# Reordering twelve attention input panels so that four attention pairs run among them, and splitting the first two output panels in halves

## The reference, cut to what matters

```
q, k, v = split(rms_norm(x) @ w_in)     # 16 query heads of 64, 4 key and 4 value heads
for each block b of 128 tokens:          # 4 blocks
    keys of block b and of block b - 1 (block 0 has none before it)
    s = q.k / 8 - slope[head] * distance, outside the band: -inf
    m = max(max(s), sink[head])
    p = exp(s - m);  denom = sum(p) + exp(sink - m)
    o = (p / denom) @ v
x = x + concat(o) @ w_out                # the output projection
x = x + swiglu(rms_norm(x))
```

## Time and profile before

| | us |
|---|---|
| median of three runs | 2536.35 |
| the profiled execution, its own time | 2536.2 |
| its span in the trace | 2534.4 |
| panel 7 to panel 11 | 2012.5 to 2041.2 |
| from panel 11's end to the first output panel | 2041.2 to 2107.3 |
| the eight output panels | 2107.3 to about 2151 |

### The profile page before, as it was taken

How to read it: one execution, slowest core, us unless ns; L and a number is a source line. 1 busy time by engine, 2 the same in 40 slices (tenths; PEclk the granted TensorE clock), 3 DMA queues, 4 the chain that set the end, 5 groups by cost and what they waited for, 6 DMA issues and landing times.

```text
span 2534.4 us, 35089 instructions
## 1 busy us (share of the span) xinstructions
PE 2441.7 (96%) x12016; PEld 2072.3 (82%) x12016; DVE 1682.5 (66%) x3142; ACT 928.1 (37%) x1319; POOL 740.1 (29%) x646
## 2 busy tenths in 40 slices
PE   6999999898999999999999999999999979999998
PEld 4877878686887888888888899999999756788886
DVE  4887769688566667677642478888887685444434
ACT  4223853523233333333333333333333464222222
POOL 0000000000006666676676257777641000000000
PEclk8999999999999999999999999999999999999999
DMA  6222913254234444444456689999997202222321
GB/s 257 100 73 93 350 34 129 95 190 159 100 111 139 139 148 141 150 138 149 139 171 193 206 295 366 365 366 362 360 363 258 76 25 67 91 99 91 100 99 58
DMA packets 177221, 433.59 MB, mean 171 GB/s; under 512 B 32752, under 2 KB 81904, under 8 KB 176752
## 3 DMA queue, kind: packets, MB, share of 16 engines
q1 hardware_dynamic: 123888, 331.61, 37.8%
q0 software_dynamic: 34816, 67.41, 7.7%
q10 hardware_dynamic: 18432, 33.56, 3.6%
HBM read 371.48 MB, written 61.01 MB: 171 GB/s over the span
## 4 chain that ended last, share of the span: by engine, by line
PE 87%; DVE 9%; ACT 2%; issue 1%; DMA 1%; SPq 0%; ACTq 0%; DVEq 0%
PE ps L466 17%; PE ps L467 17%; PE ps L468 17%; PE ps L802 9%; PE ps L803 9%; PE ps L801 9%; PE ps L712 2%; DVE wlo L1398 1%; DVE ar L1451 1%; PE ps L696 1%; PE ps L704 1%; PE ps L781 1%; DVE ar L1513 1%; ACT whi L936 1%; DVE rstd L1412 1%
## 5 line engine op out<-in xcount | busy, mean ns | idle before, releaser
L1398 DVE TENSOR_TENSOR wlo<-raw,whi 128x1024 fp32r<-128x1024 f32 x426 | 521.4, 1224 | 569.7 <-ACT whi L936 568.2
L2239 POOL DMA_INDIRECT w_scratch<-ar x384 | 418.8, 1091 | 953.5 <-DVE wlo L1398 854.3
L936 ACT ACTIVATE whi<-raw 128x1024 fp32r<-128x1024 f32 x424 | 448.9, 1059 | 660.0 <-PE ps L803 403.4
L466 PE MATMUL ps<-b_hi,whi 128*128 128x512 f32 x1328 | 519.6, 391 | 3.2 <-DVE wlo L1398 3.0
L468 PE MATMUL ps<-b_hi,wlo 128*128 128x512 f32 x1328 | 517.6, 390 | 0.0
L467 PE MATMUL ps<-b_lo,whi 128*128 128x512 f32 x1328 | 517.3, 390 | 0.0
L801 PE MATMUL ps<-a_hi,whi 128*128 128x384 f32 x1024 | 342.7, 335 | 0.0
L803 PE MATMUL ps<-a_hi,wlo 128*128 128x384 f32 x1024 | 342.1, 334 | 0.0
L802 PE MATMUL ps<-a_lo,whi 128*128 128x384 f32 x1024 | 342.1, 334 | 0.0
L466 PE MATMUL ps<-a_hi,whi 128*128 128x512 f32 x816 | 326.9, 401 | 8.9 <-DVE wlo L1398 7.2
L467 PE MATMUL ps<-a_lo,whi 128*128 128x512 f32 x816 | 319.6, 392 | 0.0
(11 more groups left out here) (265 smaller groups left out, 2988.7 us busy)
## 6 DMA issues: line engine op xcount, KB each, us to landing
raw<-panels SPq DMA_DIRECT2D x430, 512.0 KB, 3.4
gelu_scratch<-ar ACTq DMA_DIRECT2D x128, 256.0 KB, 2.1
w_scratch<-rstd SPq DMA_DIRECT2D x32, 768.0 KB, 10.9
ar<-w_scratch SPq DMA_DIRECT2D x128, 192.0 KB, 4.7
ar<-gelu_scratch SPq DMA_DIRECT2D x128, 192.0 KB, 5.6
ar<-mod SPq DMA_DIRECT2D x32, 512.0 KB, 5.6
ar<-panels SPq DMA_DIRECT2D x3, 2048.0 KB, 16.0
w_scratch<-ar POOLq DMA_INDIRECT x384
```

Of the source, the lines that this page charges most:

```text
L466: pe.matmul(bank, w_h, hi[:, k, :], start=(k == 0), stop=False)
L936: act.activation(whi[:, u % SPLIT, :], raw[:, u % RAW, :], ACT.Copy).then_inc(hi_ready, 1)
L1398: dve.tensor_tensor(wlo[:, u % SPLIT, :], raw[:, u % RAW, :], f32(whi[:, u % SPLIT, :]), ALU.subtract).then_inc(lo_ready, 1)
L2239: nc.gpsimd.indirect_dma_start(experts, bass.IndirectOffsetOnAxis(offs[:, k:k + 1], 0), vals[:, k:k + 1], None)\
```

## The change

The panels' order becomes key 0, value 0, queries 0 to 3, key 1, value 1, queries 4 to 7. From the seventh on all use bank 3, and each waits until the one before it has been taken out. Groups are ordered by kt outside and b from 3 down to 0 inside, so pairs 0 to 3 need only the first seven panels. Their work is written among panels 7 to 11, on all three engines. The first two output panels are each split into two halves of four tiles; the first halves need only the outputs of kt = 0 and are written among pairs 6 and 7. Output panels use banks 4 to 7. The maximum's three short instructions become two, with `less_sinks` made once. `v2_feat_sb` moves into `nt`.

```diff
-SWB = (0, 2, 3, 1)
+SWB = (0, 2, 3, 1, 0, 2, 3, 3, 3, 3, 3, 3)
+SW_ORDER = (0, 2, 4, 5, 6, 7, 1, 3, 8, 9, 10, 11)
-        v2_feat_sb = area(A_S2, 2, T)
+        v2_feat_sb = nt[:, :, :]
@@ SP
+            for n, w in enumerate(SW_ORDER):
+                sp.wait_ge(lo_ready, SW + n - RAW + 1 - U)
+                sp.dma_start(raw[:, (SW + n) % RAW, :], panels[SW + w]).then_inc(landed[(SW + n) % RAW], 16)
...
+            groups = [(b, kt, half) for kt in range(2) for b in reversed(range(TT)) for half in range(2)]
...
@@ PE
+            swa_panel(6)
+            swa_scores(0)
+            swa_panel(7)
             swa_scores(1)
+            swa_panel(8)
+            swa_turn(0)
+            turn_v(1, 2)
+            swa_scores(2)
+            swa_turn(1)
+            swa_panel(9)
+            swa_values(0)
+            swa_turn(2)
+            swa_scores(3)
+            swa_turn(3)
+            swa_panel(10)
+            swa_turn(4)
+            swa_values(1)
+            swa_turn(5)
+            swa_panel(11)
+            swa_turn(6)
+            pe.wait_ge(bank_free, r_of(SW) + 16)
+            swa_scores(4)
+            swa_values(2)
+            swa_turn(7)
+            swa_scores(5)
+            swa_values(3)
+            swa_turn(8)
+            swa_scores(6)
+            swa_turn(9)
+            swa_scores(7)
+            swa_turn(10)
+            swa_values(4)
+            swa_turn(11)
+            swa_turn(12)
+            swa_values(5)
+            out_half(0, 0)
+            swa_turn(13)
+            swa_turn(14)
+            swa_values(6)
+            out_half(1, 0)
+            swa_turn(15)
+            swa_values(7)
+            out_half(0, 1)
+            out_half(1, 1)
...
@@ ACT
+            for n in range(4):
+                bias_tiles(n)
+                swa_panel_hi(6 + n)
+            bias_tiles(4)
             swa_exp(0)
             swa_exp(1)
+            swa_panel_hi(10)
+            swa_exp(2)
+            swa_exp(3)
+            swa_out(0)
+            swa_panel_hi(11)
+            swa_out(1)
+            swa_exp(4)
+            swa_exp(5)
+            swa_hi(0)
+            swa_out(2)
+            swa_panel_hi(12)
+            swa_out(3)
+            swa_exp(6)
+            swa_exp(7)
+            bias_tiles(5)
+            swa_out(4)
...
+            swa_out(10)
+            swa_exp(12)
+            swa_hi(4)
+            hi_next(0, SO, 0)
...
-                dve.tensor_tensor(tiny[:, o:o + 4], tiny[:, o:o + 4], col("sinks", h, 4), ALU.max).then_inc(mx2, 1)
-                dve.wait_ge(mx2, n + 1)
-                dve.tensor_scalar(tiny[:, o + 4:o + 8], tiny[:, o:o + 4], -1.0, None, ALU.mult).then_inc(nmx2, 1)
-                dve.tensor_tensor(tiny[:, o + 12:o + 16], col("sinks", h, 4), tiny[:, o:o + 4], ALU.subtract).then_inc(nmx2, 1)
+                dve.scalar_tensor_tensor(tiny[:, o + 4:o + 8], tiny[:, o:o + 4], -1.0, less_sinks[:, h:h + 4], ALU.mult, ALU.min).then_inc(nmx2, 1)
+                dve.wait_ge(nmx2, 2 * n + 1)
+                dve.tensor_tensor(tiny[:, o + 12:o + 16], col("sinks", h, 4), tiny[:, o + 4:o + 8], ALU.add).then_inc(nmx2, 1)
...
@@ DVE, after panel 11
+            pair_bias(4)
+            swa_lo(2)
+            pair_bias(5)
+            pair_norm(4)
+            pair_bias(6)
+            swa_lo(3)
+            pair_norm(5)
+            pair_bias(7)
+            lo_next(0, SO, 0)
+            swa_lo(4)
+            pair_norm(6)
+            swa_lo(5)
+            pair_norm(7)
+            swa_lo(6)
+            swa_lo(7)
```

More of the change, by code:

```diff
@@ L175, in build @@
         tiny = sb("tiny", [P, 96])
+        less_sinks = sb("less_sinks", [P, NH2])
         sq = sb("sq", [P, 2, T])
@@ L909, in _, with out_half @@
-            pe.wait_ge(o2, len(groups) // 2 - 1)
-            strips(SO, KT, b_hi, b_lo, each=last_outputs)
+            def out_half(u, half):
+                if half == 0:
+                    pe.wait_ge(lo_ready, SO + u + (1 - U))
+                    pe.wait_ge(bank_free, r_of(SO) + u + 1)
+                    pe.wait_ge(bias2, 4 * len(groups))
+                    pe.wait_ge(o2, TT)
+                else:
+                    pe.wait_ge(o2, 2 * TT)
+                for k in range(4 * half, 4 * half + 4):
+                    last = split3(ps[:, 4 + u, :], u, k, b_hi[:, k, :], b_lo[:, k, :], k == 0, k == KT - 1)
+                if half:
+                    last.then_inc(used, 1)
@@ L912, in last_stat @@
+            out_half(1, 1)
+            for k in range(2, KT):
+                panel(SO + k, k % 4, ps[:, 4 + k % 4, :], b_hi, b_lo, r_of(SO) + k + 1)
             def last_stat(i, u):
@@ new lines, in query2, with residual @@
+            def query2(n, p):
+                dve.wait_ge(used, SW + p + 1)
+                dve.scalar_tensor_tensor(q2[:, n, :], ps[:, SWB[p], :], HD2 ** -0.5, rstd[:, :], ALU.mult, ALU.mult).then_inc(bank_free, 1)
+            def residual(first, count):
+                for n in range(first, first + count):
+                    dve.scalar_tensor_tensor(x[:, n, :], x[:, n, :], col("final1", n), rstd1, ALU.mult, ALU.mult).then_inc(y1_ready, 1)
+            swa_panel_lo(1)
+            norm_rstd(3)
@@ L2058, in _ @@
+            swa_panel_lo(2)
+            key2(0, 0)
+            swa_panel_lo(3)
+            value2(0, 1)
+            swa_panel_lo(4)
             for k in range(1, KT - 1):
                 add_sq(4, k, rstd1)
[L2060 to L2064, removed]
+            query2(0, 2)
@@ L2066, in swa_bias @@
+            value2_out(0, 4)
+            swa_panel_lo(5)
+            query2(1, 3)
+            groups = [(b, kt, half) for kt in range(2) for b in reversed(range(TT)) for half in range(2)]
             def swa_bias(n):
@@ L2118, in _, with pair_bias, pair_norm @@
[L2118 to L2121, removed]
+            def pair_bias(m):
+                swa_bias(2 * m)
+                swa_bias(2 * m + 1)
+            def pair_norm(m):
                 swa_norm(2 * m)
                 swa_norm(2 * m + 1)
[L2124 to L2128, removed]
@@ L2129, in _ @@
-            swa_lo(len(groups) // 2 - 1)
+            query2(2, 4)
+            dve.tensor_scalar(less_sinks[:, :], col("sinks", 0, NH2), -1.0, None, ALU.mult).then_inc(mx2, 1)
+            swa_panel_lo(6)
+            norm_rstd(4, rstd1)
+            query2(3, 5)
+            swa_panel_lo(7)
+            residual(0, 4)
+            key2(1, 6)
+            swa_panel_lo(8)
+            dve.wait_ge(mx2, 1)
+            dve.wait_ge(bias_ready, NH2 // 2)
+            pair_bias(0)
+            value2(1, 7)
```

176 lines of the change are left out of this document (98 added, 78 removed).

## The result

The changed kernel takes 2545.62 us, the median of six runs (2543.74 to 2546.84); before, run beside it, takes 2536.27 (six runs, 2536.1 to 2540.2). The ratio is 1.003, with a 95% interval of 1.0018 to 1.0041: slower by 9.4 us, some 5 to 10. The forecast was 2544.5 in a range of 2538 to 2549. The profiled execution took 2545.18 us, with a span of 2543.4. One of the ten executions of a later experiment, keep_warm, took 4398.79 us at a mean granted clock of 0.705 and stands in no comparison.

What follows compares the result with a forecast made beforehand. Attention was taken as a chain through three engines, none full, held back by ACT's written order. Order 5.6 later plus clock 2.6 gave 8.2 us on the profiled 2536.2, 2544.5 by the median; range 2538 to 2549.

Steps and rivals of the forecast that it cites:

- Before panel 7: Start of the stage: panel 6 ends 1.9 us earlier, as waits for a value panel and a `lo` go.
- Panels 7 to 11: Attention work among these panels: 44.8 us of PE work plus 10.9 of waits with restarts, 55.7 in all.
- turn 3: PE's wait there: exponentials 4 and 5 and the rest take ACT 5.5 us against PE's 4.1, 1.35.
- nearly 7: ACT's idle us before `hi` 11, waiting for panel 9, with a copy and exponentials behind; the same expected at `hi` 12.
- After panel 11: Rest of attention: 25.1 us of work and 18.4 of waits with restarts, 43.5 without output work.
- The clock and the sum: PE's slower clock at 5.5 places, 5.7 us against 3.1 before, adds 2.6; with 5.6 the total is 8.2 slower.
- the order's part: Attention's end, output work left out: 2109.8 against 2104.2 for before by the same reckoning, 5.6 us later.
- The first: Rival: ACT reaches copies 1 and 3 and exponentials during panels 9 and 10; 4.9 us faster, 2531.5; chance 0.11.
- The second rival: Panels around the waits keep PE's clock up: only 2.5 us slower, 2538.9; chance 0.13.
- The third: Rival: every long PE wait drops the clock: 15.3 us slower, 2551.7; chance 0.08.
- The short instruction: One of DVE's three short maximum instructions goes: 0.08 us off each group, bounds 0 to 2.7 over 16 groups.
- The one bank for panels 7 to 11: Claimed to cost nothing: DVE's taking out lies under attention work, showing only as 0.4 us at scores 4.

Runs made afterwards that it cites:

- keep_warm: Changed kernel plus 79 extra matmuls with unread results in eight PE waits of about 2 us or more; stage 197.94 us, ratio to before 1.0023.
- changed_again: The changed kernel run once more, unmodified, on another chip; stage 201.80 us, ratio to before 1.0022.
- act_order: Changed kernel with ACT's whole written order in the attention stage redone, PE and DVE untouched; stage 185.59 us, ratio to before 0.9978.
- the second pair: Both kernels, before and changed, run once more unmodified on another chip; stages 196.88 and 201.80 us.
- outs_first: Changed kernel with ACT's copies of groups 1 and 3 moved ahead of the `hi` of panels 11 and 12; stage 202.85 us, ratio to before 1.0046.
- exps_first: As outs_first, with exponentials 0 also ahead of `hi` 9 and exponentials 4 and 5 ahead of `hi` 11; stage 200.14 us, ratio to before 1.0026.
- all_order: Changed kernel with the written orders of PE, ACT and DVE in the attention stage all renewed; stage 173.13 us, ratio to before 0.9901.
- order_no_halves: As all_order, with the output panels undivided and behind the last pair; stage 175.65 us, ratio to before 0.9915.

## Why the prediction was right

**Before panel 7.** Panel 6 ends 47.7 after the first input panel began, before 49.6: 1.9 earlier, as forecast.

**Panels 7 to 11.** 57.9 against a forecast of 55.7 without the clock. The waits, forecast then measured: turn 0 0.3 and none, turn 1 2.4 and 2.94, values 0 2.25 and 2.12, turn 3 1.35 and none, turn 4 2.25 and 2.21, turn 5 2.0 and 2.03. Turn 3's is missing because values 0 in front of it ran at half speed (3.32 in place of 1.94), which used it up. In changed_again, where values 0 ran at full speed, it is there:

```profile
2097.25 1.94 PE L892 MATMUL ps<-ar 128*64 128x512 f32 x8 [2.12 <-ACT ar L1381]
...
2102.85 1.07 PE L872 MATMUL ps<-sm,ar 128*128 128x128 f32 x8 [1.54 <-ACT ar L1381]
```

ACT stood 6.79 before `hi` 11 and `hi` 12, forecast "nearly 7". That the waits come from ACT's order was argued there and is shown by act_order: the same work in 45.1. The Trainium skill (TensorE: Matmul & The Clock Gate, Architectural detail) has ScalarE strictly first in, first out; the trace agrees with it by those two waits of 6.79, in the last 5.6 of which a ready copy stood behind.

**After panel 11.** 53.0, less 5.4 of output halves, is 47.5, against 43.5 without the clock. Waits, forecast then measured: scores 4 0.4 and 0.35, scores 5 0.9 and 1.03, turn 8 4.3 and 4.32, scores 7 2.3 and 2.36, turn 10 1.3 and 1.38, turn 12 5.2 and 4.49, turn 14 1.2 and 1.21, values 7 0.8 and 0.69, the second halves 1.5 and 1.42. The forecast's end of the bias passes behind scores 6, 20.0, is 0.2 short of its own terms (14.7, 2.0 and 3.5), which moves nothing else. The third output panel starts at 2125.9, forecast near 2126.

**The clock and the sum.** The two stretches exceed their sums without a clock by 2.2 and 4.0, 6.2 together; the forecast for the clock was 5.7. Not all of it is the clock's: changed_again had 3.4 of low time among the panels in place of 6.8, and that stretch was only 0.2 shorter, since turn 3 then waited. At 0.15 to 0.32 per us the 6.9 of low time that changed has more than before are 1.0 to 2.2, where the forecast had +2.6. And this term is not a property of the kernels: in the second pair the changed kernel had less low time (13.6) than before (23.9), and its stage was only 4.9 longer, not 8.8. With the low time taken out at those prices, the order's part is 6.6 to 7.8 in the first pair and 6.5 to 8.2 in the second, where the forecast had 5.6. So the mechanism was right and its size too small by 1 to 2.6, the clock's term was too large by 0.4 to 1.6 in the first pair, and that the forecast of 8.2 came so near the measured 9.4 is in part luck. Against before on the chip of changed_again the median was 6.7 longer.

**The rivals.** The first, that panels cover the waits, was put at 2531.5, 4.9 below before, if ACT got at copies 1 and 3 and the exponentials while panels 9 and 10 ran. In the changed kernel it does not. outs_first brought the copies forward and not the exponentials, and the stage was no shorter. exps_first brought exponentials 4 and 5 forward as well and gained 2.2, where the rival wanted about 13. Only with the whole order of ACT redone did the waits among the panels go, and then the stage was 8.0 under before's. With PE and DVE reordered too the mechanism is larger than I had priced it: all_order is 20.4 under before. The Trainium skill (Perfetto Trace Analysis, Optimization Strategy) says that interleaving regimes may improve performance; the runs show both outcomes of one interleaving, +8.8 us with one written order and -20.4 with another. The second rival, the clock stays up, fell (17.1 of low time); keep_warm shows a stage 4.4 shorter with 3.4 of it left. The third, every long wait drops the clock, fell too: turn 1 waited 2.94 and turn 4 2.21, they ran in 1.06 and 1.07, and what stood behind them ran at full speed. Turn 5 waited 2.03 and ran in 1.06, but a few matmuls later the clock fell inside panel 11, where each took 0.42 from start to start in place of 0.23:

```profile
2060.73 0.63 PE L477 MATMUL ps<-a_hi,wlo 128*128 128x512 f32 x1
2061.15 0.63 PE L475 MATMUL ps<-a_hi,whi 128*128 128x512 f32 x1
```

So there were five low stretches, near the 5.5 of the forecast: four behind the seven waits of 2 us and more, and one behind a wait of 1.38 (turn 10).

**Left open.** The short instruction (bounds 0 to 2.7 us) was not resolved. The one bank for panels 7 to 11 was not tried alone; what bounds it is the wait of 0.35 at scores 4 and the 0.11 us of idle PE in 55 in all_order, which keeps it. The price of low time is known only to a factor of two, and each stage length is of one execution.

## What to carry to other kernels

When work is moved between two stages on one engine, write out the other engines' queues too: an instruction that waits for a long piece of another engine's work (here a `hi` that waits for a panel) holds everything ready that stands behind it, and moving only the first thing out from behind it mostly passes the wait on to the next. With the same pieces the order alone decided between a stage 8.8 us longer and one 20.4 us shorter, and the halves that were worth nothing in the poor order were worth 2.5 in the good one, so a part that shows no effect should be tried again once the bound has moved. Where differences are below 1% of a long program, compare the stage's length in the profile, with PE's busy, idle and low-clock time beside it.

## What the runs showed of the hardware that was not expected

The time at low clock is not fixed by the instruction stream: the same kernel, before, had 10.2 and 23.9 us of it in the same stage in two executions on two chips, and the second stage was 3.3 us longer. In the second, 13.6 us in a row were at low clock behind a wait of 2.45, with no wait above 0.8 among them. It did disappear where the idle places did: 6.8 in act_order, and none at all in all_order and order_no_halves, whose longest idle times of PE before an instruction of the stage were 1.7 and 1.8 us. The one in all_order is turn 10, at full speed behind it, in PE's timeline:

```profile
2135.79 1.07 PE L872 MATMUL ps<-sm,ar 128*128 128x128 f32 x8 [1.71 <-ACT ar L1381]
```
